# Three attentions reordered from row tiles to head pairs, with six buffers for turned probabilities

## The reference, cut to what matters

```python
# first block: 8 heads, causal, with a bias by distance          -> "attention 0"
probs = softmax(q k^T * scale + bias);  y = probs v
# second block, layer 0: 12 heads; three branches with gates     -> "attention 1"
o = g0 * softmax_compressed v_c + g1 * softmax_selected v_s + g2 * softmax_window v_w
# second block, layer 1: 12 heads of low-rank attention          -> "attention 2"
# both layers add 4 heads over 256 memory tokens                 -> last 4 heads of 1 and 2
xa = softmax(xq mem_k^T * scale) mem_v
y = concat([mix, xa]) @ w_out;  x = layer_norm(alpha x + y);  x = layer_norm(alpha x + experts(x))
```

## Time and profile before

| what | before |
|---|---|
| three runs | 1041.45, 1045.36, 1046.85 us; median 1045.36 |
| profiled execution, span | 1041.7 us |
| PE busy in the span | 999.9 us (96%) |
| DVE, ACT, POOL busy | 556.4, 404.7, 112.1 us |
| attention 0 (first scores to last values) | 63.05 to 91.57, 28.52 us |
| attention 1 | 424.96 to 474.65, 49.69 us |
| attention 2 | 760.27 to 792.22, 31.95 us |

### The profile page before, as it was taken

The page is one execution under the profiler, slowest core; times in us unless marked ns, Lnnn a source line. Parts: engine busy times, 40 slices in busy tenths (PEclk is TensorE's granted clock), DMA queues, the critical chain, the costliest instruction groups (busy, mean ns, idle before and its releaser), DMA issues.

```text
span 1041.7 us, 15492 instructions
## 1 busy us (share of the span) xinstructions
PE 999.9 (96%) x5896; PEld 677.7 (65%) x5896; DVE 556.4 (53%) x1201; ACT 404.7 (39%) x793; POOL 112.1 (11%) x149
## 2 busy tenths in 40 slices
PE   7999999999999999899999999989999999999984
PEld 7978899999876888778634434338667734344332
DVE  5756656667447744765334333547665414443454
ACT  5565456655336554672312212123483312121210
POOL 0722101111001000250002000000131002000000
PEclk9999999999999999999999999999999999999998
DMA  9873676555355535409999999995348999999992
GB/s 328 201 247 83 208 231 224 177 192 213 121 202 198 162 110 209 176 3 377 403 422 410 422 421 421 422 394 213 131 183 325 379 412 410 421 422 422 421 408 98
DMA packets 96302, 292.31 MB, mean 281 GB/s; under 512 B 11278, under 2 KB 48318, under 8 KB 72670
## 3 DMA queue, kind: packets, MB, share of 16 engines
q1 hardware_dynamic: 95534, 289.54, 73.2%
q0 software_dynamic: 688, 1.71, 0.6%
HBM read 289.98 MB, written 1.25 MB: 280 GB/s over the span
## 4 chain that ended last, share of the span: by engine, by line
PE 85%; DMA 5%; DVE 5%; ACT 2%; issue 1%; POOL 0%; SPq 0%; DVEq 0%; POOLq 0%; ACTq 0%
PE ps L1006 36%; PE ps L1442 19%; PE ps L1477 9%; DMA w<-in_moe_w_up 5%; PE ps L1159 3%; PE ps L1114 2%; PE ps L1137 2%; PE ps L1414 2%; PE ps L948 2%; PE ps L1487 1%; PE ps L1287 1%; DVE plo L1699 1%; PE ps L1525 1%; PE ps L955 1%; PE ps L1364 1%
## 5 line engine op out<-in xcount | busy, mean ns | idle before, releaser
L1699 DVE TENSOR_TENSOR plo<-w,phi 128x1024 fp32r<-128x1024 f32 (+3 forms) x147 | 177.0, 1224 | 128.2 <-ACT phi L2470 128.1
L2470 ACT CAST phi<-w 128x1024 fp32r<-128x1024 f32 (+3 forms) x147 | 148.5, 1032 | 133.7 <-PE ps L1006 122.6
L1442 PE MATMUL ps<-w,arena 128*64 128x512 f32 x472 | 135.7, 595 | 1.3 <-DMA w<-in_moe_w_up 1.3
L1006 PE MATMUL ps<-hTr,phi 128*128 128x256 f32 x472 | 131.8, 279 | 0.0
L1006 PE MATMUL ps<-yTr,phi 128*128 128x256 f32 x472 | 131.3, 278 | 0.0
L1006 PE MATMUL ps<-hTr,plo 128*128 128x256 f32 x472 | 131.2, 278 | 0.0
L2260 DVE CAST hots<-ps 128x256 fp32r<-128x256 f32 x16 | 6.8, 424 | 187.4 <-PE ps L1452 172.1
L1006 PE MATMUL ps<-phi,hTr 128*128 128x512 f32 (+2 forms) x240 | 93.8, 391 | 0.8 <-issue 0.7
L1006 PE MATMUL ps<-phi,yTr 128*128 128x512 f32 (+2 forms) x240 | 93.4, 389 | 0.0
L1442 PE MATMUL ps<-arena 128*64 128x512 f32 x280 | 89.3, 595 | 1.6 <-DMA ring<-in_moe_w_up 0.9
L1006 PEld LDWEIGHTS ps<-hTr,plo 128*128 128x128 f32 x472 | 89.5, 190 | 0.0
(11 more groups left out here) (361 smaller groups left out, 1720.9 us busy)
## 6 DMA issues: line engine op xcount, KB each, us to landing
w<-in_moe_w_down SPq DMA_DIRECT2D x37, 1024.0 KB, 16.1
w<-in_moe_w_up SPq DMA_DIRECT2D x31, 1024.0 KB, 18.9
w<-in_moe_w_gate SPq DMA_DIRECT2D x28, 1024.0 KB, 16.2
w<-in_w_up SPq DMA_DIRECT2D x22, 1024.0 KB, 7.7
arena<-in_moe_w_gate SPq DMA_DIRECT2D x18, 1024.0 KB, 14.2
arena<-in_moe_w_up SPq DMA_DIRECT2D x17, 1024.0 KB, 12.9
arena<-in_moe_w_down SPq DMA_DIRECT2D x15, 1024.0 KB, 23.2
w<-in_w_out SPq DMA_DIRECT2D x6, 2048.0 KB, 10.1
```

Of the source, the lines that this page charges most:

```text
L1006: ins_ = e.matmul(o, l[a], r[b], start=first and i == 0, stop=last and i == 2, skip_group_check=group)
L1442: ins_ = e.matmul(bank[64 * ee:64 * ee + 64, :], xg[:, k, o:o + 64], half_view(i, kind, p, ee, ab)[:, c, :], start=(k == 0), stop=(k == 7))
L1699: e.tensor_tensor(plo[:, 0:m], slots[u % 3][:, j * m:j * m + m], phi[:, 0:m].bitcast(F32), ALU.subtract).then_inc(s_cut)
L2470: e.copy(pieces[p % 4][0][:, 0:m], slots[u % 3][:, j * m:j * m + m]).then_inc(s_cast)
```

## The change

The step becomes a pair, `c`: TensorE does the scores of both its units, the turn of tile 0 of the pair before, the values of both tiles of the pair before that, and the turn of tile 1. In attention 1 the extra products of the two tiles stand side by side. `Tr` gets six buffers in the same memory. VectorE and ScalarE are rewritten to the same step; `cast` and `cut` stand at the end of steps 1 to 4, `memory_beside` goes two pieces at a time, and attention 1's `keep_on` stands ahead of the first turn and waits for the shares.

```diff
-        Tr = [Tb[0], Tb[1], Tb[2], Lb[1]]
+        Tr = [ring[:, b:b + 512] for b in range(2048, 5120, 512)]
...
 # TensorE
+                            mm.append(more + own_ if t else own_ + more)
...
+                for c in range(n + 2):
+                    if c < n:
+                        scores_of(2 * c)
+                        scores_of(2 * c + 1)
+                    if a == 0 and c < 2:
+                        memory_beside(0, 2 * c)
+                        memory_beside(0, 2 * c + 1)
+                    if a == 1 and c == 0:
+                        e.wait_ge(s_pcn, 2)
+                        turn_shares(range(4))
+                    if a == 1 and c == 1:
+                        turn_shares(range(4, 6))
+                        await_empty("pt")
+                    if a and c == 1:
+                        keep_on(psum[7], (0, 4, 3)[a])
+                    if a == 0 and c == n:
+                        e.wait_ge(s_small, 16 * 7)
+                        mixed(a, 2 * n - 2, (0, 1))
+                    if 1 <= c <= n:
+                        turn_probs(2 * c - 2)
+                    if c == (n if a else n + 1):
+                        e.wait_ge(s_ex, tiles[jobs[-1]["J"] + 1])
+                        heads_proj(a, range(1))
+                    if c >= 2:
+                        values(c - 2)
+                    if a == 0 and c == n:
+                        mixed(a, 2 * n - 1, (2, 3))
+                    if 1 <= c <= n:
+                        turn_probs(2 * c - 1)
+                    if a == 0 and 2 <= c < 4:
+                        memory_beside(1, 2 * c - 4)
+                        memory_beside(1, 2 * c - 3)
...
 # VectorE
+                for c in range(n + 2):
+                    if c < n:
+                        masks(2 * c)
+                        masks(2 * c + 1)
+                    if a == 1 and c < 2:
+                        shares((5,) if c else (1, 3))
+                    if 1 <= c <= n:
+                        keep_turned(2 * c - 2)
+                    if c < n:
+                        inverse_sums(2 * c)
...
+                    if 1 <= c <= n:
+                        keep_turned(2 * c - 1)
...
+                    if c < n:
+                        inverse_sums(2 * c + 1)
+                    if a == 0 and 1 <= c <= 4:
+                        p = first_piece("out0") + c - 1
                         cut(p, p + 1)
...
 # ScalarE
+                for c in range(n + 2):
+                    if c < n:
+                        exponents(2 * c)
...
+                    if a == 0 and c in (2, 4):
+                        memory_kept(c // 2 - 1)
+                    if 1 <= c <= n:
+                        keep_turned(2 * c - 2)
+                    if c < n:
+                        exponents(2 * c + 1)
...
+                    if c >= 2:
+                        high_out(c - 2)
+                    if 1 <= c <= n:
+                        keep_turned(2 * c - 1)
...
+                    if a == 0 and 1 <= c <= 4:
+                        p = first_piece("out0") + c - 1
                         cast(p, p + 1)
```

More of the change, by code:

```diff
@@ L238, in build @@
         ring = sb("ring", [128, 5120])
[L239 to L240 removed]
+        Lb = [ring[:, 1536:2048]]
         small = sb("small", [128, 1448])
@@ new lines, in attention, with scores_of @@
+                n = len(jobs) // 4
+                def scores_of(u):
+                    two = jobs[2 * u:2 * u + 2]
+                    if u >= 2:
+                        old = jobs[2 * u - 3]
+                        if old["S"][0][3] is None:
+                            e.wait_ge(s_ex, tiles[old["J"] + 1])
+                        else:
+                            e.wait_ge(s_mx, tiles[old["J"] + 1])
+                    for q in range(len(two[0]["S"])):
+                        for j in two:
+                            lq, kk, w, mk = j["S"][q]
+                            ins_ = e.matmul(psum[2 * (u % 2) + j["half"]][:, q * 256:q * 256 + w], lq, kk,
+                                            start=True, stop=True)
+                    ins_.then_inc(s_s, 2)
@@ new lines, in values @@
+                def values(p):
+                    claim(f"o{a}", p)
+                    ob = B.ap(f"o{a}", p)
+                    for t in range(2):
+                        two = jobs[4 * p + 2 * t:4 * p + 2 * t + 2]
+                        for i in (4 * p + 2 * t, 4 * p + 2 * t + 1):
+                            e.wait_ge(*B.empty(f"t{a}", i))
+                        mm = []
+                        for j in two:
+                            own_ = [(j["v"][q][s], turned_probs(j["J"])[:, o * 128:o * 128 + 128])
+                                    for o, (q, s) in enumerate(j["todo"])]
+                            more = j.get("extra", [])
+                            mm.append(more + own_ if t else own_ + more)
@@ L1775, in attention @@
                 jobs = attn[a]
[L1776 to L1818, removed]
-                        evac("pt", c, PcT2[c][0:NCMP, :, :], B.ap("pt", c)[0:NCMP, :].rearrange("p (h t) -> p h t", h=2))
-                    if a == 0 and u in (6, 7, 11, 12):
-                        p = first_piece("out0") + (6, 7, 11, 12).index(u)
@@ new lines, in attention, with masks @@
+                n = len(jobs) // 4
+                def masks(u):
+                    ms = unit_stats(jobs[2 * u]["J"] // 2)
+                    for i in (2 * u, 2 * u + 1):
+                        j = jobs[i]
+                        J, nq = j["J"], len(j["S"])
+                        e.wait_ge(s_s, J + 1)
+                        if u >= 4:
+                            e.wait_ge(*B.full(f"t{a}", i - 8))
+                        b, L = psum[2 * (u % 2) + j["half"]], prob(J)
+                        for q, (lq, kk, w, mk) in enumerate(j["S"]):
+                            c, m = slice(q * 256, q * 256 + w), j["half"] * nq + q
+                            if mk is not None:
+                                e.tensor_tensor_reduce(L[:, c], b[:, c], mk, 1.0, 3.0e38, ALU.add, ALU.min,
+                                                       ms[:, 0, m:m + 1]).then_inc(s_mx)
+                            else:
+                                e.tensor_reduce(ms[:, 0, m:m + 1], b[:, c], AX.X, ALU.min).then_inc(s_mx)
@@ new lines, in keep_turned, with inverse_sums @@
+                def keep_turned(u):
+                    i = 2 * u + 1
+                    J, w = jobs[i]["J"], 128 * len(jobs[i]["todo"])
+                    e.wait_ge(*B.full(f"t{a}", i))
+                    if J >= len(Tr):
+                        e.wait_ge(s_pv, J - len(Tr) + 1)
+                    e.tensor_copy(turned_probs(J)[:, 0:w], B.ap(f"t{a}", i)[:, 0:w]).then_inc(B.sem_empty(f"t{a}", i))
+                def inverse_sums(u):
+                    two = jobs[2 * u:2 * u + 2]
+                    nq = len(two[0]["S"])
+                    ms = unit_stats(two[0]["J"] // 2)
+                    e.wait_ge(s_ex, tiles[two[1]["J"] + 1])
+                    gates = two[0].get("gates")
+                    if gates is None:
+                        e.reciprocal(ms[:, 2, 0:2 * nq], ms[:, 1, 0:2 * nq]).then_inc(s_rc)
+                    else:
+                        own.step(e.reciprocal(ms[:, 2, 0:2 * nq], ms[:, 1, 0:2 * nq]))
+                        settle()
+                        r4 = ms[:, 2, :].rearrange("p (h q) -> p h q", h=2)
+                        e.tensor_tensor(r4, r4, gates, ALU.mult).then_inc(s_rc)
```

168 lines of the change are left out of this document (70 added, 98 removed).

## The result

The changed kernel takes 1044.26 us in the median of 16 runs; the kernel before 1040.85 in 16, of which three are the runs that were known ahead and the others ran beside it. One of the 16 runs of the changed kernel was a slow one of 2664.26 us, which the ratio leaves out; the median of the other 15 is 1044.11. The ratio is 1.0032, 95% interval 1.0017 to 1.0046: slower by a third of a per cent, some 3.3 us. The forecast was 0.5 us less than before, and the sign is wrong. The time lies where the rival "the clock falls" put it (+2.9).

The account below looks back on a forecast made before the run. TensorE was taken to bound the attentions. Attention 0's +1.2, attention 1's -0.5 and attention 2's -1.2 with its passing on gave -0.5 us: 1044.9 against a median of 1045.36, range 1039.7 to 1049.5.

Parts of the forecast that it names:

- the clock falls: Rival: TensorE's clock drops behind both new gaps in attentions 0 and 1, 1.7 us each, total +2.9 us; chance 0.15.
- the sum of -0.5: Whole kernel, no clock drop: +1.2 from attention 0, -0.5 from attention 1, -1.2 from attention 2 with its release.
- Group change: TensorE, all attentions: each change of matmul kind costs 0.16 to 0.24 us; pairs fall from 5.65 to 5.3, -6.0 together.
- No merging gain: Rival: the price sits with waits, not kinds, so +6.0 - 0.5 us; chance 0.11 together with waits in every step.
- Attention 0: TensorE waits about 3.1 us, 0.3 before unit 1's turn, the rest before unit 3's; merging saves 1.9: +1.2 us.
- Attention 1: Gap of some 2.7 us before the filler; merging -2.2, beginning +1.1, tail's wait +0.6: -0.5 us.
- 441.3: Attention 1's beginning: the time in us when pair 0's values end, against 440.28 before; the beginning costs +1.1.
- Pairs in the middle don't wait: Attentions 1 and 2; rival: ten middle pairs wait 0.6 us each on bank 4, +6; chance 0.11 with no gain.
- Attention 2: Merging saves 1.9 us, unit 14's turn waits 1.1, 0.9 more than before: -1.0 us.
- Passing on: Expert-stage loads, released in attention 2 by unit 11's values, move by -1.7 us, the next release by -1.0; taken as -1.2.
- forecast alone: Range of the median if the forecast itself holds, its sum within 2.5 us: 1041.5 to 1047.5 us; chance 0.57.
- Clean saving: Rival: `cut` and the shares hold nobody up, only the tails' waits stand against the merging saving: -4.7 us; chance 0.17.

Follow-up runs that it names:

- after_again: The changed kernel unaltered, run again for a second profile and more times; ratio 1.0029 to the kernel before.
- new_in_0: The new order in attention 0 only, the order of the kernel before (with six buffers) in attentions 1 and 2; ratio 1.0031 to the kernel before.
- shares_first: Changed kernel with attention 1's last share copy between the masks of units 2 and 3, filler in an earlier-free bank; ratio 0.9970 to the kernel before.
- cut_later: Changed kernel with `cast` and `cut` of the four projection pieces one step later, steps 2 to 5, in attention 0; ratio 0.9994 to the kernel before.
- new_in_1: The new order in attention 1 only, the order of the kernel before in attentions 0 and 2; ratio 1.0016 to the kernel before.
- gaps_fitted: Changed kernel with six calls of a useless filling matmul in each of TensorE's two new waits; ratio 0.9989 to the kernel before.
- both_again: A repeat of both_fixed, the same kernel, beside another kernel on one chip; ratio 0.9929 to the kernel before.
- both_fixed: Changed kernel with the edits of cut_later and shares_first together, and `mkT` taken out behind its step's first keeping; ratio 0.9964 to the kernel before.
- gaps_filled: Changed kernel with twelve calls of a useless filling matmul in each of TensorE's two new waits; ratio 1.0049 to the kernel before.
- new_in_2: The new order in attention 2 only, the order of the kernel before (with six buffers) in attentions 0 and 1; ratio 1.0011 to the kernel before.

## Why the prediction was wrong

**The step that failed** is the clock: "by the rows, which show no drop after the shorter gaps, -0.5". That sum put the drop at nothing and gave the rival a chance of 0.15. The profiles have eight places with one of the two gaps idle (attention 0: the changed kernel, after_again, new_in_0, shares_first; attention 1: the changed kernel, after_again, cut_later, new_in_1), and the clock fell at seven of them, towards the end of the wait or behind it. Where a gap was filled or taken away, or the order of before stood, ten places in each attention, it never fell inside an attention. The gaps of 1.2 to 1.4 us in the earlier trace rows, at full clock, were no evidence for gaps twice as long. The rule that was weighed there (the Trainium skill, TensorE: Matmul & The Clock Gate, "HAM oscillation": after gaps the gate throttles again and the work behind them pays) forecast the right way. The trace agrees at seven of the eight places, with 0.50 granted behind waits of 2.65 and 2.78 us; that section speaks of longer gaps than these. The price was near the 1.7 us a piece that the rival took from the earlier trace rows: 1.15 to 2.5 in attention 0, 1.4 to 1.7 in attention 1. With these prices the sum of -0.5 becomes about +2 to +3.7, and 3.3 was measured.

**What held.** With the clock kept up, as in gaps_fitted, the forecast comes out: attentions of 29.46, 49.65 and 31.00 us against 29.7, 49.2 and 30.9, and -1.1 us (-3.3 to +1.1) against -0.5.

- Group change: a pair at 5.31 us, forecast 5.3. The saving over a whole attention is seen where the waits are gone. In attention 1 of both_again: -2.2 forecast, the 1.18 us before the first turn of the earlier trace rows gone, a new wait of 0.38 and the tail's 0.24 to pay: -2.8; measured 46.86 - 49.69 = -2.8. In attention 0: -1.9, and 0.25 and 0.59 of waits left: -1.1; measured -1.1. "No merging gain" falls. The new wait of attention 1 and the second one of attention 0, in both_again:

```profile
431.96 1.18 PE L1125 MATMUL ps<-cst,ring 128*128 128x128 f32 x8 [0.38 <-ACT ring L2561]
79.62 0.66 PE L1125 MATMUL ps<-cst,ring 128*128 128x128 f32 x4 [0.59 <-ACT ring L2561]
```

- Attention 0: forecast 0.3 and 2.8 us of wait, measured 0.25 and 2.65, by the path that was named: `cast`, `cut`, masks, exponents, `mkT`, keeping.
- Attention 1: gap of 2.7 forecast, 2.78 measured. The attention itself came out 0.5 longer than the forecast with the clock kept, though its tail was cheaper, 0.24 instead of 0.6. The forecast counted the merging of the beginning twice: its 441.3 is built from the merged groups' prices, and the -2.2 for the whole attention has the same groups again. In gaps_fitted the beginning costs +1.3 (forecast +1.1; its own terms, 441.3 - 440.28, give +1.0), and what follows saves 1.4 after the tail's 0.24, so 1.6 of the 2.2. Pairs in the middle don't wait, so that rival falls.
- Attention 2: wait before the turn of unit 14 forecast 1.1 us, measured 0.80. Unit 13's turn, which waited 0.17, now shows no wait; unit 11's shows one of 0.19. The turns of units 11 and 14:

```profile
787.99 0.66 PE L1125 MATMUL ps<-cst,gain_rows 128*128 128x128 f32 x4 [0.19 <-ACT ring L2557]
792.64 0.66 PE L1125 MATMUL ps<-cst,gain_rows 128*128 128x128 f32 x4 [0.80 <-ACT ring L2557]
```

- Passing on: the load queue's wait in attention 2 shrank from 28.0 us by 1.5 (forecast 1.7):

```profile
SPq L861 <- PE ps L1144: 26.5, 1, 26.5
```

That the expert stage then takes more from it than the 1.0 us of attention 2 itself, 1.2 in the forecast, is not shown: from the end of attention 2 to the end of the span the changed kernel's two profiles took 247.2 and 248.4 us, before's 249.5, and new_in_0, with before's attention 2, 248.2. The scatter is larger than these 0.2 us, so whether the stage moves with the release of its loads stays open.

The range "forecast alone", 1041.5 to 1047.5, does not follow from 1044.9 and 2.5 us either way, which give 1042.4 to 1047.4; nothing else hangs on it.

"Clean saving" was wrong about the changed kernel, and is what both_fixed comes near once the two places are mended: -4.9 us in the attentions, -3.8 measured, against its -4.7.

## What to carry to other kernels

Cost a new idle stretch of the bounding engine at its wait plus the clock behind it: here 2.7 us of wait cost 1.15 to 2.5 us more at half clock at seven of eight places, and that turned a small gain into a loss. When units are merged, look at what stands between the units on the other engines: `cut`, which held nobody before, came to stand ahead of masks that TensorE waits for, and a share copy that TensorE had already waited for (1.18 us) came to stand behind masks. Moving them by one place, with a filler that waits for no copy, was worth 7 us (1.0032 against 0.9964, each against its own runs of before). Idle time that can't be removed can be filled with matmuls of no use (0.9989 against 1.0029), as long as the fill isn't longer than the wait.

## What the hardware showed unexpectedly

The feed-forward products of 128x256 run at one of two spacings through a whole stretch in these profiles. The same group of the changed kernel's two profiles, 140 to 220 us (count, busy us, mean ns), first the one shown above:

```profile
L1008 PE MATMUL ps<-hTr,phi 128*128 128x256 f32 x228 | 64.2, 281 | 0.0
```

and after_again:

```profile
L1008 PE MATMUL ps<-hTr,phi 128*128 128x256 f32 x236 | 65.1, 276 | 0.0
```

With the two groups like it, 682 such products lie in those 80 us in one execution and 708 in the other, both at full clock and without a wait: 117.3 and 113.0 ns each, some 4.7 us over the 1080 products of the stretch. Of the 14 profiles six were at the slow spacing (both_fixed among them, both_again not), so a kernel alone does not set it; it widens the scatter of the runs. What does set it was not tried.

The lower clock needs no idle stretch either: before shows it in dense work, shortly after 24 products of 30 columns each:

```profile
415.02 2.76 PE L1330 MATMUL ps<-small,arena 128*128 128x30 f32 x24
```

So do three of the twelve experiments' profiles at that place (gaps_filled, both_again, new_in_2); the others have the same products and no drop. None of the profiles with the lower clock in attention 1 has it there as well; the runs don't tell whether the one replaces the other.
